# Cross attention woven head by head into the gemms around it

## The reference, cut to what matters

```python
def cross_attention(h, mem_h, wq, wkv, wo):      # XA_HEADS = 4, head dim 256, 256 memory rows
    q = (h @ wq).reshape(B, S, XA_HEADS, XA_HEAD_DIM)
    k, v = jnp.split(mem_h @ wkv, 2, axis=-1)    # computed ahead, in the mixer
    s = jnp.einsum('bshd,bmhd->bhsm', q, k).astype(jnp.float32) * (XA_HEAD_DIM ** -0.5)
    p = jax.nn.softmax(s, axis=-1).astype(v.dtype)
    o = jnp.einsum('bhsm,bmhd->bshd', p, v).reshape(B, S, D_MODEL)
    return o @ wo
x = x + cross_attention(rmsnorm(x, xa_norm[layer]), rmsnorm(mem, xa_mem_norm[layer]), ...)
```

## Time and profile before

| | |
|---|---|
| median of 3 runs | 2882.45 us (2880.85 to 2892.63) |
| the profiled execution: time, span | 2886.11 us, 2884.3 us |
| mean granted TensorE clock | 0.975 |
| TensorE busy | 2724.6 us (94%) |
| VectorE busy | 1819.3 us (63%) |
| ScalarE busy | 1410.9 us (49%) |
| weight loads | 836 of 512 KB, 155 GB/s read over the span |

### The profile page before, as it was taken

The page is one execution under the profiler, slowest core; times in us unless marked ns, Lnnn a source line. Parts: engine busy times, 40 slices in busy tenths (PEclk is TensorE's granted clock), DMA queues, the critical chain, the costliest instruction groups (busy, mean ns, idle before and its releaser), DMA issues. The chain is left out here.

```text
span 2884.3 us, 48970 instructions
## 1 busy us (share of the span) xinstructions
PE 2724.6 (94%) x21046; PEld 2631.0 (91%) x21046; DVE 1819.3 (63%) x2346; ACT 1410.9 (49%) x1924; POOL 0.2 (0%) x4
## 2 busy tenths in 40 slices
PE   7998989999998898999999999979999899999998
PEld 7998889999997878999888999979988899889998
DVE  5657656656656646666655765877554785655764
ACT  5445545454456354544445455544455544445443
POOL 0000000000000000000000000000000000000000
PEclk9999999999999999999999999999999999999999
DMA  6553435555543124455444455325542465444463
GB/s 211 176 190 126 162 109 194 183 190 184 189 146 114 59 96 146 162 187 190 159 153 134 154 198 162 109 66 191 193 154 95 143 198 190 152 163 137 154 196 128
DMA packets 129000, 450.09 MB, mean 156 GB/s; under 512 B 20112, under 2 KB 20368, under 8 KB 128528
## 3 DMA queue, kind: packets, MB, share of 16 engines
q1 hardware_dynamic: 128784, 446.96, 47.2%
HBM read 445.47 MB, written 1.44 MB: 155 GB/s over the span
## 5 line engine op out<-in xcount | busy, mean ns | idle before, releaser
L260 PE MATMUL B<-R,WH 128*128 128x256 f32 x10432 | 2105.4, 284 | 61.9 <-DVE R L956 37.1
L260 PEld LDWEIGHTS B<-R,WH 128*128 128x128 f32 x10432 | 1695.1, 191 | 76.6 <-DVE R L956 27.5
L890 DVE TENSOR_TENSOR WL<-SL,WH 128x1024 fp32r<-128x1024 f32 x836 | 1011.3, 1223 | 796.4 <-ACT WH L1888 795.4
L260 PE MATMUL B<-R,WL 128*128 128x256 f32 x4480 | 1267.1, 283 | 0.0
L1888 ACT ACTIVATE WH<-SL 128x1024 fp32r<-128x1024 f32 x836 | 866.4, 1053 | 576.3 <-PE B L260 475.8
L260 PEld LDWEIGHTS B<-R,WL 128*128 128x128 f32 x4480 | 857.3, 191 | 0.0
L260 PE MATMUL B<-RB,WH 128*128 128x256 f32 x1984 | 556.4, 280 | 0.0
L260 PE MATMUL B<-RB,WL 128*128 128x256 f32 x1728 | 482.5, 279 | 0.0
L260 PEld LDWEIGHTS B<-RB,WH 128*128 128x128 f32 x1984 | 373.6, 188 | 0.4 <-DVE WL L890 0.2
L260 PEld LDWEIGHTS B<-RB,WL 128*128 128x128 f32 x1728 | 324.0, 187 | 0.0
L260 PE MATMUL B<-WH,R 128*128 128x512 f32 x480 | 159.6, 402 | 3.1 <-DVE WL L890 3.0
(11 more groups left out here) (280 smaller groups left out, 1522.5 us busy)
## 6 DMA issues: line engine op xcount, KB each, us to landing
SL<-in_w SPq DMA_DIRECT2D x836, 512.0 KB, 3.5
CP<-in_cp SPq DMA_DIRECT2D x5, 768.0 KB, 4.9
X<-in_xT SPq DMA_DIRECT2D x2, 512.0 KB, 6.6
PG<-in_mem SPq DMA_DIRECT2D x1, 1024.0 KB, 10.8
out<-X SPq DMA_DIRECT2D x1, 1024.0 KB, 3.9
PK<-in_pk SPq DMA_DIRECT2D x1, 594.5 KB, 3.8
dn_y<-PG SPq DMA_DIRECT2D x1, 256.0 KB, 4.1
PG<-dn_y SPq DMA_DIRECT2D x16, 16.0 KB, 2.0
```

The costliest lines, as they stand in the source:

```text
L260: return p.matmul(o, left, right, start=first, stop=final, skip_group_check=True)
L890: v.tensor_tensor(WL[t % NSPL][:, :], SL[t % NRAW][:, :], WH[t % NSPL][:, :].bitcast(F32), ALU.subtract).then_inc(s_lo, 1)
```

## The change

A unit is now one head with all 256 tokens. TensorE does scores of heads 0, 1, 2 ahead of blocks 18, 20, 26 of the query gemm and transposes of heads 0, 1 ahead of blocks 28, 30; behind the gemm follow values 0, scores 3, transposes 2, values 1, values 2; transposes 3 and values 3 go into the output gemm, ahead of its blocks (0, 2) and (0, 4). The output gemm takes its groups 0 and 1 in turn, block by block. VectorE no longer subtracts the maximum: it multiplies the maximum by -1/16 (128 x 2), and ScalarE does the exponential straight from PSUM with that as its bias, in two instructions of 256, and then gives the bank back. ScalarE copies a head's transposes with one instruction instead of two. The order of VectorE's and ScalarE's programs follows.

```diff
-        outer = 2 if name in ("c.o", "g.o") else OUTER if ...
+        outer = 2 if name in ("c.o", "g.o", "xo0", "xo1") else OUTER if ...
...
 tensor_program, cross:
-                through(normed(f"xq{layer}", n))
-                for j in range(4):
-                    evacuated(f"xq{layer}", j)
                 def scores(u):
                     bk = small(("xs", layer, u))
+                    evacuated(f"xq{layer}", u)
+                    for tb in range(2):
                         for c in range(2):
+                            f = 2 * u + c
+                            t = mm(bk[:, cc(tb)], Q[:, f * 256 + tb * 128:f * 256 + tb * 128 + 128], K[:, cc(f)], c == 0, c == 1)
                     t.then_inc(s_small, 1)
...
+                def values(head):
                     bk = small(("xo", layer, head))
-                    freed(("xpt", layer, 2 * (head // 2)))
-                    freed(("xpt", layer, 2 * (head // 2) + 1))
+                    freed(("xpt", layer, head))
...
+                for j, k in normed(f"xq{layer}", n):
+                    x = 8 * j + k
+                    if x in (18, 20, 26):
+                        scores(x // 4 - 4 if x < 26 else 2)
+                    if x in (28, 30):
+                        weights(x // 2 - 14)
+                values(0)
+                scores(3)
+                weights(2)
+                values(1)
+                values(2)
                 for j, k in gemm(f"xo{layer}", R45, R45, 0, 2048):
+                    if (j, k) == (0, 2):
+                        weights(3)
+                    if (j, k) == (0, 4):
+                        values(3)
                     if j == 0 and k % 2 == 0:
                         freed(("xo", layer, k // 2))
...
 vector_program, cross:
                 def scores(u):
                     m = mx[:, 2 * u:2 * u + 2]
                     bk, _ = had(("xs", layer, u))
                     v.reduce_max(m, r3(bk[:, :]), AX).then_inc(V.sem, V.up())
                     v.wait_ge(V.sem, V.n)
-                    v.tensor_tensor(r3(SS[:, hc(u)]), r3(bk[:, :]), m.unsqueeze(2).broadcast_to([128, 2, 256]),
-                                    ALU.subtract).then_inc(free, 1)
+                    v.tensor_scalar(m, m, -1.0 / 16, None, ALU.mult).then_inc(xmax.sem, xmax.give((layer, u)))
 
                 def weights(u):
                     S, m = r3(SS[:, hc(u)]), sm[:, 2 * u:2 * u + 2]
-                    v.wait_ge(xexp.sem, xexp[layer, u])
+                    freed(("xs", layer, u))
...
+                for j, k in walk(name, n):
+                    x = 8 * j + k
+                    for y in due(name, j, k, True):
+                        v.wait_ge(s_rst, n + 1)
+                        scaled_to(name, y, Q)
+                    if x in (19, 21, 27):
+                        scores(x // 2 - 9 if x < 27 else 2)
+                    if x in (25, 28):
+                        weights(x // 28)
+                scores(3)
+                weights(2)
+                rest(0)
+                weights(3)
+                rest(1)
+                rest(2)
+                rest(3)
                 add_to_x(f"xo{layer}", n + 1, 1.0, gain)
...
 scalar_program, cross:
+                def exps(u):
+                    a.wait_ge(xmax.sem, xmax[layer, u])
+                    bk, free = had(("xs", layer, u))
+                    for tb in range(2):
+                        t = a.activation(SS[:, u * 512 + tb * 256:u * 512 + tb * 256 + 256], bk[:, cc(tb)], ACT.Exp,
+                                         bias=RT2[:, 2 * u + tb:2 * u + tb + 1], scale=1.0 / 16)
+                    t.then_inc(free, 1)
 
                 def weights(u):
                     bk, free = had(("xpt", layer, u))
+                    a.activation(PT[:, :, u, :], r3(bk[:, :]), ACT.Copy).then_inc(free, 1)
...
+                for j, k in walk(f"xq{layer}", n):
+                    x = 8 * j + k
+                    if x in (22, 23):
+                        exps(x - 22)
+                    if x == 28:
+                        exps(2)
+                    if x in (29, 31):
+                        weights(x // 31)
+                exps(3)
+                weights(2)
+                for head in range(3):
+                    high_part(head)
+                weights(3)
+                high_part(3)
                 add_to_x(f"xo{layer}", n + 1, gain)
```

More of the change, by code:

```diff
@@ L74, in stage_table @@
     for name, kc, groups, width in rows:
-        outer = 2 if name in ("c.o", "g.o") else OUTER if name in ("f1.0.in", "r0.q", "c.in", "g.qk", "r3.q") or name.endswith(".up") else 0
+        outer = 2 if name in ("c.o", "g.o", "xo0", "xo1") else OUTER if name in ("f1.0.in", "r0.q", "c.in", "g.qk", "r3.q") or name.endswith(".up") else 0
         table[name] = Stage(name, kc, groups, width, block, turn, outer)
@@ L233, in build_program @@
         ab_or = Signal(sem("s_ab_or"), ["or"])
-        xexp = Signal(sem("s_xexp"), [(layer, u) for layer in range(2) for u in range(4)])
+        xmax = Signal(sem("s_xmax"), [(layer, u) for layer in range(2) for u in range(4)])
         xw = Signal(sem("s_xw"), [(layer, u) for layer in range(2) for u in range(4)])
@@ L467, in weights @@
                     for mc in range(2):
-                        for hh in range(2):
-                            at = (2 * mc + hh) * 128
-                            t = p.transpose(bk[:, at:at + 128], S[:, hh * 256 + mc * 128:hh * 256 + mc * 128 + 128], IDN)
+                        for tb in range(2):
+                            at = u * 512 + tb * 256 + mc * 128
+                            t = p.transpose(bk[:, (2 * mc + tb) * 128:(2 * mc + tb + 1) * 128], SS[:, at:at + 128], IDN)
                     t.then_inc(s_small, 1)
[L472 to L478, removed]
+                def values(head):
                     bk = small(("xo", layer, head))
-                    freed(("xpt", layer, 2 * (head // 2)))
-                    freed(("xpt", layer, 2 * (head // 2) + 1))
+                    freed(("xpt", layer, head))
                     for c in range(2):
@@ L1202, in cross @@
                 name = f"xq{layer}"
[L1203 to L1206, removed]
                 def scores(u):
                     m = mx[:, 2 * u:2 * u + 2]
-                    bk, free = had(("xs", layer, u))
+                    bk, _ = had(("xs", layer, u))
                     v.reduce_max(m, r3(bk[:, :]), AX).then_inc(V.sem, V.up())
                     v.wait_ge(V.sem, V.n)
-                    v.tensor_tensor(r3(SS[:, hc(u)]), r3(bk[:, :]), m.unsqueeze(2).broadcast_to([128, 2, 256]),
-                                    ALU.subtract).then_inc(free, 1)
+                    v.tensor_scalar(m, m, -1.0 / 16, None, ALU.mult).then_inc(xmax.sem, xmax.give((layer, u)))
                 def weights(u):
                     S, m = r3(SS[:, hc(u)]), sm[:, 2 * u:2 * u + 2]
-                    v.wait_ge(xexp.sem, xexp[layer, u])
+                    freed(("xs", layer, u))
                     v.reduce_sum(m, S, AX).then_inc(V.sem, V.up())
@@ L1224, in weights, with rest @@
                                     ALU.mult).then_inc(xw.sem, xw.give((layer, u)))
[L1225 to L1231, removed]
+                def rest(head):
                     bk, free = had(("xo", layer, head))
                     part_lo(f"x{layer}", head, bk[:, :]).then_inc(free, 1)
+                for j, k in walk(name, n):
[14 more added lines that the diff above has]
+                rest(3)
                 add_to_x(f"xo{layer}", n + 1, 1.0, gain)
@@ L2143, in cross, with high_part @@
                 PT = PG[9][:, :].rearrange("p (m h t) -> p m h t", m=2, h=4)
[L2144 to L2149, removed]
+                def exps(u):
+                    a.wait_ge(xmax.sem, xmax[layer, u])
+                    bk, free = had(("xs", layer, u))
+                    for tb in range(2):
+                        t = a.activation(SS[:, u * 512 + tb * 256:u * 512 + tb * 256 + 256], bk[:, cc(tb)], ACT.Exp,
+                                         bias=RT2[:, 2 * u + tb:2 * u + tb + 1], scale=1.0 / 16)
+                    t.then_inc(free, 1)
                 def weights(u):
-                    hp, tb = u // 2, u % 2
                     bk, free = had(("xpt", layer, u))
[L2154 to L2163, removed]
+                    a.activation(PT[:, :, u, :], r3(bk[:, :]), ACT.Copy).then_inc(free, 1)
+                def high_part(head):
                     bk, free = had(("xo", layer, head))
                     part_hi(f"x{layer}", head, bk[:, :])
+                for j, k in walk(f"xq{layer}", n):
[12 more added lines that the diff above has]
+                high_part(3)
                 add_to_x(f"xo{layer}", n + 1, gain)
```

5 lines of the change are left out of this document (removed).

## The result

The changed kernel took 2894.6 us (median of 20 runs) against 2886.2 of the kernel before (20 runs). The ratio is 1.0026 (the medians alone give 1.0029), 95% interval 1.0016 to 1.0036: 0.26% slower, inside the 0.5% that I had called no change. The profiled execution has a span of 2893.6 against 2884.3. (The interval here is narrower than that 0.5%, so the sign is measured too.)

A forecast was written before the change was run, and what follows sets the result against it. TensorE, busy 94% of the span, bounds the kernel, so only its waits and low clock count. Full clock -0.3 plus low clock 8.3 made +8 us, 2890 us by the median 2882.45; own range 2884 to 2897, 8 in 10 2873 to 2901.

The forecast's parts named there:

- the two gaps: Between query and output gemm, both layers: 56.4 us in all; 15.7 us of work a layer, 25 us saved without waits.
- Stall 1: Inside the query gemm, TensorE waits 2.4 us for head 1's weights, which stand behind a tile conversion on VectorE.
- Stalls 2 and 3: Between the gemms, TensorE waits 2.95 us ahead of head 2's transposes and 2.2 us ahead of head 1's values.
- V3 at T = 421.0: Inside the output gemm of layer 0, head 3's values start on TensorE at 421.0 us.
- The tail: From head 3's values to the next norm's squares' sum: 30.1 us, with TensorE waits of 0.6, 2.1 and 2.3.
- The rival of a free tail: Chance 0.20: the chain behind head 3's values has slack and TensorE keeps what it gained; -3 us, 2879.
- The pair of groups: Behind head 3's values, VectorE takes groups 0 and 1 of X together, each 2.22 us with its hand-overs.
- Full clock, -0.3: Change of both layers' stages at full clock, stalls and tail included: -1.2 + 0.9 = -0.3 us.
- Clock, +8.3: Low clock behind stall 1 (0.85), stalls 2 and 3 (1.9) and the next gemm's start (1.4): 4.15 us a layer.
- The clock stays low throughout: Rival, chance 0.12: from stall 1 until near head 3's values full clock is not granted again; +16 us, 2898.
- The clock holds: Rival, chance 0.15: the stalls come as told but the clock is never low; 2882 us.
- What costs nothing: VectorE's small multiply, ScalarE's exponential from PSUM and single weights copy: no added time, bounds -1 to +1 us in all.

The follow-up runs named there:

- e9: e8 with VectorE taking head 2's weights ahead of the first early conversion and ScalarE copying head 3's transposes ahead of the second; ratio 0.9906 to the kernel before.
- e7: e3 with VectorE also taking head 1's weights ahead of the tile conversion due at block 28; ratio 0.9920 to the kernel before.
- e2: Changed kernel with head 2's weights and copy and head 0's parts ahead of head 3's maximum and exponential on VectorE and ScalarE; ratio 0.9975 to before.
- e5: Changed kernel with extra matmuls, results overwritten, keeping TensorE at work in stalls 1 to 3; ratio 0.9995 to the kernel before.
- e1: Changed kernel with the output gemm's first three tile conversions moved ahead, out from behind head 3; ratio 1.0012 to the kernel before.
- e3: Changed kernel with the edits of e1 and e2 together; ratio 0.9953 to the kernel before.
- e10: e7 with head 2's weights ahead of VectorE's first early conversion and head 3's copy ahead of ScalarE's second, groups still in turn; ratio 0.9931 to before.
- e4: Changed kernel with the output gemm group by group again instead of groups 0 and 1 in turn; ratio 0.9997 to the kernel before.
- e8: e7 with the output gemm group by group and the third early conversion back in its place; ratio 0.9942 to the kernel before.

## Why the prediction was right

*Nothing to gain but the two gaps; 15.7 us of work in each; 25 us at most.* This held. e9, in which next to nothing waits, gained 23.3 in the distances and 27 in the runs (22 to 32 by its interval). With the work alone it would be 75.8 - 29.3 + 15.7 = 62.2 us from sum to sum, and 63.2 were measured.

*Stall 1, 2.4.* It was 2.23 and 2.28. Its cause, the weights behind the conversion at block 28, is shown by e7.

*Stalls 2 and 3, 2.95 and 2.2.* They were 2.59 and 1.97. Part of the difference is in how they are counted: I took work off the distance between starts, and a row counts its idle time from the modelled end of the last matmul. By distances of starts, in layer 1, stall 2 is 2.75 and stall 3 is 2.14. What is left of stall 2, 0.2, is in the hand-overs (the sum starts 0.08 behind the small multiply, for which I had 0.2). That the order of the queues causes both is shown by e2.

*V3 at T = 421.0, which is 44.6 behind the sum at 376.39.* It was 44.3 with the clock kept up (e5).

*The tail, 30.1 from V3 to sum.* It was 29.8 in layer 1 and 29.9 in e5, and 31.3 in layer 0. I had its three waits at 0.6, 2.1 and 2.3; the first came as 1.69 in layer 0 and 0.22 in layer 1, the others as 1.73 and 2.02. The 1.4 too little in layer 0 is one transfer: it landed 4.6 us after its issue, where I had 3.0 to 3.5. Three conversions in a row free three buffers, and three transfers are issued within 2.3 us, but this alone does not explain it. The same three are issued as closely in layer 1 and in both layers of e2 and e5, and there the first landed after 3.1 or 3.2 us, and only the second and third after 4.1 to 5.0. Why it was slow in this one place stays open. With it the output gemm ended some 42.5 us behind the query gemm in layer 0, outside the 38 to 41 that I had named as a sign, and some 40.3 in layer 1 (estimates from the last tile's first block, at 444.50 and 1187.42). The rival of a free tail is out: in e1 the same work took 26.8.

*The pair of groups.* I had it as one of the terms that feed the tail. The experiments show it as a bound of its own: the wait is 2.0 in e1, e3, e7 and e10 whatever was done early, and by group it is 1.11 in e4 and 0.67 in e8 and e9. The traces show why. From the start of the pair on VectorE to the norm's sum on TensorE it is 19.7 us in the changed kernel (437.96 to 457.68) and just as long in e1 and e10. VectorE idles in these only in the hand-overs to and from ScalarE. In e1 and e10 it had even waited 2.59 us for work just ahead of the conversion in front of the pair, so it was not late.

*Full clock, -0.3.* It was -1.2 (148.4 in e5 against 149.6).

*Clock, +8.3: 0.85, 1.9 and 1.4 a layer.* Between sum and V3 the low clock cost 6.9 in both layers together, where I had 5.5. Stall 1 had a low stretch behind it in layer 0 and none in layer 1, as the half chance has it. What I had too small is stalls 2 and 3: they cost 2.5 in layer 1, where nothing else before V3 was low, instead of 1.9. Behind the start of the next gemm there was a low stretch in layer 1 and none in layer 0. It cost at most 1.7 in all instead of 2.8, and it lies behind the sum, so outside these distances.

*The sum, +8.* The forecast for the distances alone is -0.3 + 5.5 = +5.2, and they grew by -1.2 + 6.9 + 1.3 (the transfer) = +7.0. With the clock behind the sum it is +8 against at most 8.7, and the span's +9.3 holds differences between executions as well. The ratio that I forecast, 2890 to 2882.45, is the measured 1.0026 to the last digit, though the time itself, 2894.6, is 4.6 above the 2890 that I gave, as the kernel before came out higher too (2886.2 by 20 runs). The mechanism was right, but a match that close is luck: four errors of 0.9 to 1.4, two up and two down, nearly cancel.

*The clock stays low throughout.* It did not; in layer 0 the full clock was granted again between stalls 1 and 2, from 406 to 412.5. *The clock holds.* It did not either; e5 shows what that would have given, 0.9995.

*What costs nothing.* The exponential's pair from PSUM took 0.84 instead of the 0.66 that I read off the copies; in the changed kernel no wait of TensorE goes back to it. TensorE waited for no tile inside the query gemm.

Two things are not settled. One is whether W2 between stalls 2 and 3 counts for the clock (the Trainium skill's statement on transposes, TensorE: Matmul & The Clock Gate, Part 4: PE-mode transpose), as e5 put plain matmuls there and no run took W2 alone. The other is the 2.3 us outside the two stages, of which the clock behind the sum of layer 1 can be up to 1.7; the rest is within what single executions differ by.

## What to carry to other kernels

Work woven into a busy engine's gaps is only as early as its place in the *other* engines' queues: here the same instructions were 0.26% slower or 0.94% faster, by where a few of them stood in the queues and in which order the output gemm's groups came. Before a gap is closed, list what the other engines did for later in its shelter, and move that first. Where groups are made to finish together, their readers come as one piece: put the time from that piece to the next thing that waits for them into the sum.

## What the runs showed of the hardware

A wait of 2.2 to 2.3 us for the weights of head 1 (stall 1) was followed by a stretch at 1.2 GHz in 6 of 10 places: in layer 0 of all five kernels that have it unfilled (the changed one and e1 to e4), and in layer 1 of e4 alone. Waits of 2.6 and 2.0 us with 0.5 us of transposes between them (stalls 2 and 3 unfilled) were followed by one in all six places (the changed kernel, e1 and e4), while the first wait of 3.12 in layer 1 of the kernel before was not. Filling the stalls with matmuls whose results nobody reads kept 2.4 GHz and saved 8 us in the distances (9 in the runs) without shortening one wait. Transfers of 512 KB landed after 3.3 us in the median of seven in the tail of e1. Where three were issued within 2.3 us (the changed kernel, e2 and e5, both layers), the first landed after 3.1 to 3.2 us in five of six places and after 4.6 in one, the second and third after 4.1 to 5.0.
